# Output bias as a product on TensorE, GpSimd's gate groups moved, ten adaLN chunks preloaded

## The reference, cut to what matters

```
mod = silu(c) @ ada_w[l] + ada_b[l]          # 6 x 1024: sh1 sc1 g1 sh2 sc2 g2
h = rmsnorm(x, g) * (1 + sc1) + sh1
layer 0: m = silu(layernorm(causal_conv31(glu(h @ w_in + b_in)))) @ w_out + b_out
layer 1: m = stick_breaking_attention(h) @ w_o
x = x + g1 * m
h = rmsnorm(x, g') * (1 + sc2) + sh2
x = x + g2 * peer(h)
```

## Time and profile before

| what | us |
|---|---|
| device time, median of 3 executions | 2995.14 (2995.13 to 2999.14) |
| device time of the profiled execution | 2995.64 |
| its span | 2993.8 |
| PE busy | 2789.6 (93%) |
| DVE busy | 2291.0 (77%) |
| POOL busy | 1761.8 (59%) |
| ACT busy | 521.5 (17%) |

### The profile page before, as it was taken

How to read it: one execution, slowest core, us unless ns; L and a number is a source line. 1 busy time by engine, 2 the same in 40 slices (tenths; PEclk the granted TensorE clock), 3 DMA queues, 4 the chain that set the end, 5 groups by cost and what they waited for, 6 DMA issues and landing times.

```text
span 2993.8 us, 46968 instructions
## 1 busy us (share of the span) xinstructions
PE 2789.6 (93%) x14854; PEld 1973.5 (66%) x14854; DVE 2291.0 (77%) x4869; ACT 521.5 (17%) x1264; POOL 1761.8 (59%) x1701
## 2 busy tenths in 40 slices
PE   7998889999999999999899988879999999999996
PEld 5776777666666666666678857766666666555553
DVE  3999998888888866666872665988888887666677
ACT  2123216100000000000243162260000000000001
POOL 0030559677777767665620461677777777777774
PEclk8998998999999999999899999989999999999999
DMA  8645455899999999999953312339999999999997
GB/s 330 241 148 219 155 209 180 338 410 410 410 410 410 409 410 410 409 409 393 363 217 127 141 57 99 135 128 393 410 409 410 410 410 409 410 410 410 410 410 317
DMA packets 242817, 957.27 MB, mean 320 GB/s; under 512 B 26952, under 2 KB 27128, under 8 KB 225016
## 3 DMA queue, kind: packets, MB, share of 16 engines
q0 software_dynamic: 147456, 536.94, 45.4%
q1 hardware_dynamic: 95224, 418.64, 35.9%
HBM read 953.37 MB, written 2.10 MB: 319 GB/s over the span
## 4 chain that ended last, share of the span: by engine, by line
DMA 29%; issue 20%; PE 18%; POOL 12%; DVE 11%; ACT 2%; DVEq 1%; POOLq 1%; ACTq 0%
DMA v_rows<-in_pk_v,idx_now 19%; DMA u_rows<-in_pk_u,idx_now 9%; PE acc L799 8%; POOL v_rows L605 5%; POOL u_rows L599 4%; PE acc L791 4%; DVE mod_rows L1963 3%; DVE u_rows L1935 1%; PE acc L1152 1%; POOL idx_now L594 1%; PE out_e L1121 1%; POOL mod_rows L670 1%; PE mid L936 1%; POOL region L671 1%; PE mid L1121 1%
## 5 line engine op out<-in xcount | busy, mean ns | idle before, releaser
L1152 PE MATMUL acc<-h_t,weights 128*128 128x256 f32 x4096 | 934.7, 381 | 0.0
L1152 PEld LDWEIGHTS acc<-h_t,weights 128*128 128x128 f32 x4096 | 778.0, 191 | 207.7 <-issue 114.5
L605 POOL DMA_INDIRECT v_rows<-in_pk_v,idx_now x456 | 622.5, 1365 | 328.5 <-DVE mod_rows L1963 192.0
L1963 DVE SCALAR_TENSOR_TENSOR mod_rows<-v_rows,dots_acts,mod_rows 128x1024 f32<-128x1024 f32 x454 | 583.8, 1286 | 255.7 <-DMA v_rows<-in_pk_v,idx_now 247.1
L599 POOL DMA_INDIRECT u_rows<-in_pk_u,idx_now x512 | 643.5, 1257 | 198.0 <-issue 142.5
L1935 DVE SCALAR_TENSOR_TENSOR u_rows<-u_rows,h_rows 128x1024 f32<-128x1024 f32 x512 | 626.3, 1224 | 168.0 <-DMA u_rows<-in_pk_u,idx_now 161.9
L1169 PE MATMUL out_e<-weights,mod_rows 128*128 128x512 f32 x1024 | 469.9, 602 | 27.8 <-DVE mod_rows L2031 27.7
L1169 PEld LDWEIGHTS out_e<-weights,mod_rows 128*128 128x128 f32 x1024 | 190.9, 191 | 233.5 <-issue 200.6
L799 PE MATMUL acc<-h_t,weights 128*128 128x256 f32 x1024 | 238.6, 395 | 13.3 <-ACT h_t L1376 8.8
L1169 PE MATMUL out_e<-weights,c_pad_room 128*128 128x512 f32 x512 | 233.1, 599 | 11.7 <-DVE c_pad_room L2031 11.7
L799 PEld LDWEIGHTS acc<-h_t,weights 128*128 128x128 f32 x1024 | 201.8, 199 | 47.4 <-ACT h_t L1376 9.4
(11 more groups left out here) (272 smaller groups left out, 2800.5 us busy)
## 6 DMA issues: line engine op xcount, KB each, us to landing
weights<-in_u_t SPq DMA_DIRECT2D x256, 512.0 KB
weights<-in_v_t SPq DMA_DIRECT2D x256, 512.0 KB, 6.8
weights<-in_pk SPq DMA_DIRECT2D x32, 1024.0 KB, 4.8
v_rows<-in_ada SPq DMA_DIRECT2D x30, 1024.0 KB, 6.5
weights<-in_w_qkv SPq DMA_DIRECT2D x24, 1024.0 KB, 4.9
weights<-in_w_in SPq DMA_DIRECT2D x16, 1024.0 KB, 7.8
weights<-in_ada SPq DMA_DIRECT2D x8, 1024.0 KB, 4.9
weights<-in_w_out SPq DMA_DIRECT2D x8, 1024.0 KB, 4.8
```

Source lines behind the costliest of these rows:

```text
L605: nc.gpsimd.indirect_dma_start(v_rows[:, r % VR, :], None, a["pk_v"], bass.IndirectOffsetOnAxis(ap=idx_now[:, 1, par, r:r + 1], axis=0)).t ...
L1152: last = nc.tensor.matmul(acc[s][:, 0:HALF], weights[:, s, k * P:(k + 1) * P], h_t[:, k, :], start=k == 0, stop=k == KB - 1)
L1963: stt_op(out=y, in0=v_rows[:, r % VR, :], scalar=acts[:, bass.ds(b * BATCH + r, 1)], in1=y, op0=ALU.mult, op1=ALU.add).then_inc(v_used, 1)
```

## The change

Three edits, independent of each other.

1. The bias is added in `conv_out`: each of its eight chunks begins with one more matmul, a row of ones (1 x 128) times a row of b_out (1 x 256, seen twice, so 512 columns), into the same accumulator; the product then already holds the bias, and `residual` multiplies it with g1. `add_bias`, its semaphore and the broadcast load go; b_out is a load of 4 KB into a row of `region`.
2. GpSimd makes the one-hots of groups 11, 19, 26 and 31 in place of 6, 14, 22 and 30. Sets 2 and 3 stand behind row 0 and row 1 of the interleaved batch in place of rows 1 and 3.
3. `LATE` is 2 and `SPARES` 10. Slot 6 is in `mod_rows`, slots 7 and 8 are further parts of `region`, slot 9 is in `u_rows`; the last three are loaded only when GpSimd has looked up all of half 0. `SPARES_AT` says behind which query chunk each load is issued.

```
-LATE, SPARES = 6, 6
+LATE, SPARES = 2, 10
+SPARES_AT = ((0, 6), (1,), (2,), (3, 7), (4, 8), (5, 9), (), ())
...
+        spare_slots = ([region[:, at:at + CHUNK] for at in (0, 2048, 4336, 6384, 12800, 14848)] + [mod_rows[:, D:D + CHUNK]] +
+                       [region[:, at:at + CHUNK] for at in (8432, 10480)] + [u_rows[:, 4:6, :].rearrange("p r n -> p (r n)")])
+        AFTER_RANKS = (7, 8, 9)
...
-        b_out_rows, bias_rows = h_rows[:, 0, :], h_rows[:, 1, :]
+        b_out_row = region[0:1, 8704:9728]
...
+        POOL_AT = (11, 19, 26, 31)
+        ITERS = len(POOL_AT)
...
         def by_pool(n):
-            return n % EIGHTH == BY_POOL
+            return n in POOL_AT
...
-                    sp.dma_start(b_out_rows, a["b_out"].partition_broadcast(P)).then_inc(b_out_in, 16)
+                    sp.dma_start(b_out_row, a["b_out"].rearrange("(o n) -> o n", o=1)).then_inc(b_out_in, 16)
...
-                if at[:3] == ("pk", 0, 1) and at[3] < SPARES:
-
-                    sp.dma_start(spare_slots[at[3]], a["ada1"][ADA_CHUNKS - LATE - SPARES + at[3], :, :]).then_inc(spare_in[at[3]], 16)
+                for i in (SPARES_AT[at[3]] if at[:3] == ("pk", 0, 1) else ()):
+                    if i in AFTER_RANKS:
+
+                        sp.wait_ge(looked_up, PK[0, 0] + PH)
+                    sp.dma_start(spare_slots[i], a["ada1"][ADA_CHUNKS - LATE - SPARES + i, :, :]).then_inc(spare_in[i], 16)
...
-            def eighth_hots(l, j):
-
-                n = j * EIGHTH + BY_POOL
+            def pool_hots(l, j):
+
+                n = POOL_AT[j]
                 if j:
-                    pool.wait_ge(gates_full, l * ROUNDS * GROUPS + CREDIT + n - EIGHTH + 1)
+                    pool.wait_ge(gates_full, l * ROUNDS * GROUPS + CREDIT + POOL_AT[j - 1] + 1)
...
-            add_bias()
...
-                    both(q, 0, 0, (q, 1), {1: lambda: eighth_hots(l, 2), 3: lambda: eighth_hots(l, 3)})
+                    both(q, 0, 0, (q, 1), {0: lambda: pool_hots(l, 2), 1: lambda: pool_hots(l, 3)})
...
-            def by_token(stage, l, h, i, lhs):
+            def by_token(stage, l, h, i, lhs, bias=None):
                 w, to = chunk_in(stage, l, h, i)
+                if bias is not None:
+
+                    nc.tensor.matmul(to[:, :].rearrange("p (t n) -> p t n", t=2), ones_row[0:1, :],
+                                     bias[0:1, i * NC:(i + 1) * NC].unsqueeze(1).to_broadcast([1, 2, NC]), start=True, stop=False)
...
-                if (l, i) == (0, 0):
-                    dve.wait_ge(bias_added, h + 1)
```

More of the change, by code:

```diff
@@ L258, in build @@
         ada_slots = [v_rows[:, i:i + 2, :].rearrange("p r n -> p (r n)") for i in range(0, VR, 2)]
-        spare_slots = [region[:, at:at + CHUNK] for at in (0, 2048, 4336, 6384, 12800, 14848)]
+        spare_slots = ([region[:, at:at + CHUNK] for at in (0, 2048, 4336, 6384, 12800, 14848)] + [mod_rows[:, D:D + CHUNK]] +
+                       [region[:, at:at + CHUNK] for at in (8432, 10480)] + [u_rows[:, 4:6, :].rearrange("p r n -> p (r n)")])
+        AFTER_RANKS = (7, 8, 9)
         now = ([weights[:, i, :] for i in range(2)] +
@@ L410, in build @@
         block = ctx.enter_context(nc.Block())
-        EIGHTH = 8
-        ITERS = GROUPS // EIGHTH
+        POOL_AT = (11, 19, 26, 31)
+        ITERS = len(POOL_AT)
         EARLY = 5
-        BY_POOL = EIGHTH - 2
         OWN = GROUPS - ITERS
+        OWN_GROUPS = [n for n in range(GROUPS) if n not in POOL_AT]
         SLOTS = len(e_acts)
@@ L426, in own_no @@
         def own_no(n):
-            return n // EIGHTH * (EIGHTH - 1) + n % EIGHTH - (n % EIGHTH > BY_POOL)
+            return n - sum(m < n for m in POOL_AT)
         def group_of(m):
-            return m // (EIGHTH - 1) * EIGHTH + m % (EIGHTH - 1) + (m % (EIGHTH - 1) >= BY_POOL)
+            return OWN_GROUPS[m]
         def by_pool(n):
-            return n % EIGHTH == BY_POOL
+            return n in POOL_AT
         def dense_no(l, g, i=0):
@@ L748, in _ @@
                         u_row(q, 0, 0, r)
-                    eighth_hots(l, 0)
+                    pool_hots(l, 0)
                     for r in (4, 5, 6, 7):
                         u_row(q, 0, 0, r)
-                    eighth_hots(l, 1)
-                    both(q, 0, 0, (q, 1), {1: lambda: eighth_hots(l, 2), 3: lambda: eighth_hots(l, 3)})
+                    pool_hots(l, 1)
+                    both(q, 0, 0, (q, 1), {0: lambda: pool_hots(l, 2), 1: lambda: pool_hots(l, 3)})
                     both(q, 1, 1, (q, 2))
@@ L791, in by_token @@
                         last = nc.tensor.matmul(to[:, tt * NC:(tt + 1) * NC], lhs(k, tt), w[:, k * NC:(k + 1) * NC],
-                                                start=k == 0, stop=k == KB - 1)
+                                                start=k == 0 and bias is None, stop=k == KB - 1 and (bias is None or tt == 1))
                 last.then_inc(acc_full, 1)
@@ L919, in conv_out @@
                     pe.wait_ge(silu_ready, 2 * h + 1)
+                    if h == 0:
+                        pe.wait_ge(b_out_in, 16)
                 def lhs(k, tt):
@@ L924, in lhs @@
                     return c_ts[h][:, k, tt * P:(tt + 1) * P]
-                by_token("out", 0, h, i, lhs)
+                by_token("out", 0, h, i, lhs, b_out_row)
             def score(l, h, i, bank=None):
@@ L1128, in first_gates @@
                     if by_pool(n):
-                        pe.wait_ge(pool_hots_ready, l * ITERS + n // EIGHTH + 1)
+                        pe.wait_ge(pool_hots_ready, l * ITERS + POOL_AT.index(n) + 1)
                         ones, twos = pool_hot1, pool_hot2
```

1 line of the change is left out of this document (removed).

## The result

| | before | after |
|---|---|---|
| device time, median of 9 executions each | 2997.0 us (2995.1 to 2999.1) | 3003.85 us (3000.9 to 3005.9) |
| span of the profiled execution | 2993.8 | 3003.1 |

The ratio is 1.0021, with a 95% interval of 1.0012 to 1.0031: some 6 us slower (3.6 to 9.3), where 7 us faster was forecast. The loss is small. It is clear of no change and of the forecast range; whether it is more than the 0.2% (6.0 us) that was taken as the limit of the measurement, its interval leaves open.

The account below looks back on a forecast made before the run. The prediction took the transfers, full at 409 GB/s in the expert layers, as the bound, so only an earlier start helps. Terms -1.6 + 0 + 0.8 - 6.2 = -7.0 us gave 2988.1 us, range 2984 to 2993.5.

Parts of the forecast that it names:

- The step that failed: Gate rows, both layers: GpSimd's set 3 takes 9.8 us in layer 0 and 10.0 in layer 1, ahead of group 31.
- The first rival: "The transfers don't begin earlier": GpSimd's late set or half-clock groups eat most of the gain; 2990 to 2994, chance 0.32.
- the forecast's own sum: Whole kernel: -1.6 (edit 1), 0 (edit 3), +0.8 (edit 2, layer 0), -6.2 (edit 2, layer 1), together -7.0 us.
- the gain of 1.6 us for edit 1: Layer 0's output product: TensorE's waits of 0.88 and 2.54 us go, the added matmuls cost 1.84.
- The half-clock group: Gate groups at half clock: up to four, 3.3 us, in layer 0, or 2 us in layer 1; 0 in the sum.
- The bias product: Output product: 0.46 us per added matmul, 1.8 us for half 0's four; half 1's four lie beside VectorE's `rank`.
- The upper bound of 0.9: Output product: the most one added bias matmul was taken to cost, twice 0.46 us, at half the clock.
- TensorE's share of the 8.4 us: Conv stage: VectorE gains 8.4 us without `add_bias`, but TensorE gains 3.4 and no more; the rest ends in VectorE's wait.
- edit 3 at nothing: Late adaLN chunks: TensorE ends them about 11 us earlier, then waits for VectorE; 0, bounds 2 us either way.
- the held-back rows: GpSimd's two v and three u rows, issued behind set 3 in layer 0; five issues end at 535.5, before the place comes free.
- the full stretches: Expert layers with transfers at their 409 GB/s ceiling: they keep their length and end earlier only if they begin earlier.
- the late rows: Rival, both layers: the held-back rows come late and delay VectorE and later gathers; at 18 us 3002, chance 0.04.

Follow-up runs that it names:

- the change, VectorE stands: All three edits, with VectorE waiting before its last dot products until GpSimd's set 3 is complete; 2996.85 us, 1.0002 to the kernel before.
- edit 2, VectorE stands: The kernel before with only edit 2, VectorE waiting before its last dot products until GpSimd's set 3 is complete; 2995.07 us, 0.9999 to before.
- edit 1 alone: The kernel before with only the bias as a float32 product on TensorE; 2997.41 us, 1.0002 to before.
- edit 3 alone: The kernel before with only ten late adaLN chunks preloaded; 2997.10 us, 1.0001 to before.

## Why the prediction was wrong

**The step that failed** is in edit 2: "Set 3 took 9.35 us before; between that and 10.4 I take 9.8", applied in both layers. It measured 13.93. The mechanism was right: group 31 ends the row, GpSimd's set is what it waits for, and `u_block` and `v_block` stand behind it. The first rival even named it. But both bounds of the set's length came from rows of places where VectorE was making first one-hots. The move put the set under other work of VectorE, and a duration doesn't move along with its instruction. The case was in hand: in the earlier trace rows GpSimd's `tensor_tensor` and VectorE's operations with two operands in SBUF stretch each other. I used those rows for VectorE's gain in edit 1 and never asked in edit 2 what VectorE does from 525 us on. The trace of before shows it, and that GpSimd had ended (524.11) when it began:

```profile
526.25 1.21 DVE L1935 SCALAR_TENSOR_TENSOR u_rows<-u_rows,h_rows 128x1024 f32<-128x1024 f32 x1
...
528.54 0.68 DVE L1980 TENSOR_TENSOR scratch<-iota_keys,mod_rows 128x512 f32<-128x512 f32 x1
```

The Trainium skill states this (SBUF — State Buffer, "Who interferes with whom"): VectorE and GpSimd share one pair of ports, and a VectorE instruction with two SBUF inputs contends with a GpSimd instruction that reads SBUF. The traces agree: 2.56 and 2.35 us in place of 0.59 and 0.57 under such work, 0.58 under work with one operand in PSUM. Put into the forecast's own sum, the 4.1 us for each set turn -7.0 into +1.2, and the lower clock behind it, 2.6 us in each layer, into +6.4. That this is so near to the measured 6 us is in part luck, as the sum still holds the gain of 1.6 us for edit 1, which did not come either.

**The half-clock group** was not in the sum; the first rival had 2 us for it in layer 1 and, for layer 0, the first gates only. It came in both, 2.6 us each. The length of the hole alone does not tell when it comes: behind waits of 1.70 and 2.40 us (the change, VectorE stands) group 31 took 1.98 and 1.97 us, behind 2.42 and 2.41 us (edit 2, VectorE stands) 1.15. Together the two terms, 4.1 + 2.6 us, account for the 6.4 us by which layer 0's `v_block` missed (81.3 us from the first gates, where 74.9 was forecast) and for most of the 7.6 us in layer 1 (77.4 against 69.8).

**The bias product** was priced at 0.46 us from the earlier trace rows, "eight matmuls of 512 columns in the first `v_block`". Those eight are records, two for each float32 product; the output chunk of the earlier trace rows had the same price in it (7.06 us for 16 products of 256 columns, 0.88 for 512). It measured 1.05 to the next matmul and 1.22 in the chunk's length. The upper bound of 0.9 was below both. And the four in half 1 were costed at nothing with VectorE's `rank` as cover; they lengthen TensorE's row by 4.9 us there, of which not all is left at the late chunks. So of the term of -1.6 us the trace shows nothing: half 0's output product became 0.7 us longer, not 1.6 shorter. The time of edit 1 alone, +0.6 us (-2.1 to +3.3), can't tell the two apart.

**What held.** VectorE's durations in the conv stage, within 0.01 us; that only TensorE's share of the 8.4 us counts; edit 3 at nothing, with its idle stretch; no wait at group 6; the held-back rows without harm that the trace shows (the five issues end at 541.5, 6 us later than forecast, and the v row behind them still waits 4.74 us for its place, 11.47 before); the full stretches at their length. The half-clock rule of the Trainium skill (TensorE: Matmul & The Clock Gate, "What's actually happening") that was weighed against edit 3 did show: after the wait of 8.99 us the first two gate groups take 3.71 us together. Before the change they took 1.42 and 1.97 us, so little was lost by it, and edit 3 alone is 1.0001.

**Of the rivals,** "the transfers don't begin earlier" had the place right, but its bounds kept it at a gain of 1 us or more. The only rival on the slow side, the late rows, had the wrong mechanism.

## What to carry to other kernels

A duration read from a trace belongs to what the neighbouring engine was doing at that time. When an instruction of GpSimd is moved, look first at what VectorE runs in its new place, and count each stretch of operations with two SBUF operands as time in which GpSimd operations that read SBUF hardly advance (here three operations in 6.3 us in place of 1.75). If another engine waits for such work at the end of a row, count the slack backwards from the last place: here one or two groups decided between 6 us slower and 7 us faster. A product on TensorE is priced by a row of the same type per source matmul, not per record. Where TensorE is the bound it counts, however busy the other engines look beside it.

## What the runs showed that was not expected

- GpSimd `tensor_scalar` operations of 128x128 and 128x64 float32 took 0.59 and 0.57 us alone and 2.3 to 2.6 us each under back-to-back VectorE operations with two SBUF operands; VectorE's own were stretched by 0.1 us at most (0.77 for 0.68). In the earlier trace rows it was VectorE whose operations doubled and more, beside GpSimd's long ones (four in 11.64 us); GpSimd's first, of the same shape, took 11.25 us by itself. Which engine loses differs, so a blocked stretch has to be priced for both.
- A float32 product with one row of K and 512 columns takes 1.05 us at full clock, and two bf16 ones of the same shape 0.53 us together; the chunk that holds them becomes 1.22 and 0.71 us longer. A product of K = 1 is no cheaper than one of K = 128 (0.88 us for 512 columns in the output chunk).
- After the 7 us hole the lower clock (1.2 GHz) held through group 31 and into the `u_block`, some 5.5 us of work (an estimate from the granted clocks of 0.50 up to 539.4 and 0.62 from there to 541.4). After a wait of 2.42 us in layer 0 (edit 2, VectorE stands) group 31 and `u_block` kept 1.15 and 3.72 us; after one of 2.41 us in layer 1 they took 1.15 and 5.41, and after one of 1.70 us in the change with the same wait of VectorE 1.98 and 4.47.
